# Second-kind layers: who scales the wide part of the fourth batch's probabilities

## The reference, cut to what matters

```python
def hybrid_layer(x, ...):
    z = rms_norm_2(x, norm_g) @ w_in
    o_a = fox_attention(...)    * silu(f_gate)     # 4 heads, causal, with decay
    o_b = conformer_conv(...)   * silu(c_gate)     # 31 taps, layer norm, silu, product
    o_c = nsa_attention(...)    * silu(n_gate)     # 8 heads in 2 groups of 4
    return x + concatenate([o_a, o_b, o_c]) @ w_out

# inside the attentions, for every head and every query token q:
p = softmax(scores[q, keys <= q])                  # masked
o = p @ v
# nsa: o = gate0 * o_compressed + gate1 * o_selected + gate2 * o_window
```

## Time and profile before

| what | value |
|---|---|
| median of three executions | 1596.06 us |
| the profiled execution | 1593.2 us |
| its span, first to last instruction | 1591.4 us |
| TensorE busy | 1577.7 us, 99% |
| VectorE busy | 1058.8 us, 67% |
| ScalarE busy | 832.8 us, 52% |
| GpSimd busy | 259.6 us, 16% |

### The profile page before, as it was taken

One profiled execution on the slowest core, in us unless ns is written; L12 is line 12 of the kernel. 1 busy time (PEld: TensorE's weight loads), 2 busy tenths in 40 slices (PEclk: granted clock), 3 DMA queues, 4 the chain that ended last, 5 costly groups with the idle time before them and its releaser, 6 DMA issues.

```text
span 1591.4 us, 27283 instructions
## 1 busy us (share of the span) xinstructions
PE 1577.7 (99%) x11244; PEld 1434.2 (90%) x11244; DVE 1058.8 (67%) x1263; ACT 832.8 (52%) x1143; POOL 259.6 (16%) x207
## 2 busy tenths in 40 slices
PE   9999999999999999999999999999999999999998
PEld 9999888898989999999988889899999998879886
DVE  5555557865865555655565777576555589978996
ACT  5443456753454444544455665345444475757584
POOL 0000061010000000000015001000000039804960
PEclk9999999999999999999999999999999999999999
DMA  7657565442555655556746543355665557146712
GB/s 255 215 186 226 185 194 160 129 155 83 183 185 186 209 185 185 178 196 204 236 159 195 159 152 107 119 176 166 207 201 187 169 164 237 58 140 192 232 34 93
DMA packets 207813, 273.99 MB, mean 172 GB/s; under 512 B 18822, under 2 KB 168168, under 8 KB 207208
## 3 DMA queue, kind: packets, MB, share of 16 engines
q1 hardware_dynamic: 207576, 272.67, 53.7%
q10 hardware_dynamic: 144, 0.00, 0.0%
HBM read 271.61 MB, written 1.08 MB: 171 GB/s over the span
## 4 chain that ended last, share of the span: by engine, by line
PE 96%; DVE 2%; ACT 1%; issue 0%; POOL 0%; POOLq 0%; ACTq 0%; DVEq 0%
PE bank L571 30%; PE bank L620 15%; PE bank L1063 9%; PE bank L1052 7%; PE bank L2128 6%; PE bank L1256 4%; PE bank L1338 3%; PE bank L2106 3%; PE bank L2381 3%; PE bank L2281 1%; PE bank L1198 1%; PE bank L1034 1%; PE bank L1171 1%; PE bank L2213 1%; PE bank L2240 1%; PE bank L1138 1%
## 5 line engine op out<-in xcount | busy, mean ns | idle before, releaser
L483 DVE TENSOR_TENSOR wlo<-raw,whi 128x2048 fp32r<-128x2048 f32 (+1 forms) x255 | 576.5, 2264 | 307.1 <-ACT whi L472 306.6
L472 ACT ACTIVATE whi<-raw 128x2048 fp32r<-128x2048 f32 (+2 forms) x257 | 482.8, 1881 | 277.1 <-PE bank L620 102.1
L571 PE MATMUL bank<-hT_hi,whi 128*128 128x256 f32 x1408 | 390.7, 277 | 0.0
L571 PE MATMUL bank<-hT_lo,whi 128*128 128x256 f32 x1408 | 389.6, 277 | 0.0
L571 PE MATMUL bank<-hT_hi,wlo 128*128 128x256 f32 x1408 | 389.5, 277 | 0.0
L571 PEld LDWEIGHTS bank<-hT_lo,whi 128*128 128x128 f32 x1408 | 265.0, 188 | 0.0
L571 PEld LDWEIGHTS bank<-hT_hi,whi 128*128 128x128 f32 x1408 | 264.3, 188 | 0.3 <-DVE wlo L446 0.2
L571 PEld LDWEIGHTS bank<-hT_hi,wlo 128*128 128x128 f32 x1408 | 264.3, 188 | 0.0
L620 PE MATMUL bank<-whi,Y 128*128 128x512 f32 (+1 forms) x748 | 224.5, 377 | 0.0
L620 PEld LDWEIGHTS bank<-whi,Y 128*128 128x128 f32 x748 | 140.1, 188 | 27.9
L326 POOL TENSOR_TENSOR st<-st 128x1 f32<-128x1 f32 x17 | 14.0, 833 | 914.4 <-ACT X L319 914.4
(11 more groups left out here) (411 smaller groups left out, 2837.9 us busy)
## 6 DMA issues: line engine op xcount, KB each, us to landing
raw<-in_ffn_w SPq DMA_DIRECT2D x131, 1024.0 KB, 5.3
raw<-in_w_in SPq DMA_DIRECT2D x80, 1024.0 KB, 5.3
raw<-in_w_out SPq DMA_DIRECT2D x16, 1024.0 KB, 4.9
raw<-in_w_br_na SPq DMA_DIRECT2D x4, 1024.0 KB, 5.0
raw<-in_w_br_mla SPq DMA_DIRECT2D x4, 1024.0 KB, 5.0
raw<-in_w_br_gla SPq DMA_DIRECT2D x4, 1024.0 KB, 5.0
raw<-in_cmp_k_w SPq DMA_DIRECT2D x4, 1024.0 KB, 5.4
raw<-in_cmp_v_w SPq DMA_DIRECT2D x4, 1024.0 KB, 6.1
```

The lines of the kernel that those rows point to most:

```text
L472: act.activation(m["whi"][:, slot, 0:w], m["raw"][:, slot, 0:w], ACT.Copy).then_inc(s.hi_ready, 1)
L483: dve.tensor_tensor(m["wlo"][:, slot, 0:w], m["raw"][:, slot, 0:w], m["whi"][:, slot, 0:w].bitcast(F32), ALU.subtract).then_inc(s.lo_ready, 1)
L571: mm = pe.matmul(B[bank][:, mt * T:(mt + 1) * T], a, b, start=(n == 0 and k == 0), stop=(n == KK - 1 and k == 2))
```

## The change

Batch 3 joins the batches whose wide part ScalarE scales. VectorE's `prob.3` no longer issues line 2734, and ScalarE gets a step `prob.3` between `turn.7` and `exp.12`. It holds for both second-kind layers.

```diff
@@ -1945,7 +1945,7 @@ ACT2
-    ln_square tall.8 turn.7 exp.12 turn.8 exp.13 turn.9 exp.14 ln_tanh turn.10-11 out.1 ln_high hi.22 turn.12-14 hi.23
+    ln_square tall.8 turn.7 prob.3 exp.12 turn.8 exp.13 turn.9 exp.14 ln_tanh turn.10-11 out.1 ln_high hi.22 turn.12-14 hi.23
@@ -1963,7 +1963,7 @@
-WIDE_ON_SCALAR = (1, 2)
+WIDE_ON_SCALAR = (1, 2, 3)
```

## The result

The changed kernel takes 1599.02 us at the median (1595.22 to 1600.02, nine executions), against 1594.58 us for the kernel before in the same series (1593.49 to 1596.32, nine). The ratio is 1.0023, 95% interval [1.0015, 1.0032]: 3.7 us slower, 2.4 to 5.1 us by the interval (the two medians alone differ by 4.4). The forecast was 3.20 us more, or 1599.3 us in all, counted from a base of 1596.06 us. With nine executions that base stands at 1594.58, 1.5 us lower.

What follows compares the result with a forecast made beforehand. The prediction took TensorE as the bound (busy 99% of the span), with no slack against ScalarE's queue at `value.2`. Removed 0, added 1.60 us per layer over two layers: 1596.06 + 3.20 = 1599.3 us, range 1595.9 to 1600.9.

Steps and rivals of the forecast that it cites:

- The removal is worth 0: VectorE's `prob.3`: dropping line 2734, 1.22 us per layer, saves nothing because `ln.0` behind it waits for TensorE.
- 1.60 us added per layer: ScalarE's queue between `turn.7` and `exp.12`: four added activations delay `turn.8`, and so `value.2`, by 1.60 us.
- The wait at `turn.9` lies inside the one at `value.2`: TensorE: `turn.9` starts 0.44 us late for batch 3's wide part, which adds nothing to the delay of `value.2`.
- rival 3: TensorE: the new wait at `turn.9` adds to the one at `value.2`; 4.1 us slower, 1600.1 us; chance 8 in 100.
- So nothing behind `value.2` adds to the delay: TensorE after `value.2`: blocks run with inputs ready, other engines move along, so 1.60 us per layer neither grows nor shrinks.
- the cover at `turn.12`: Slack between the end of VectorE's `prob.4` and TensorE's loads of `turn.12`: claimed to grow from 0.81 to 1.04 us.
- The time in all, 1599.3 us: Whole kernel: median of three timed executions, 1596.06 us, plus 3.20 us.
- The sign for the first output product: Second layer, line 2381 on TensorE: start moves from 1556.31 by 3.20 us to 1559.51.
- Rival 1: TensorE's hidden waits further on take the delay back; between nothing and about 2.5 us left, 1596.1 to 1598.6; chance 17 in 100.
- Rival 2: VectorE's queue decides at `turn.12`, so its saving counts: up to 2.44 us faster, 1593.6 us; chance 5 in 100.
- The difference of the two engines' times alone: Scaling batch 3's wide part, priced by rule only: 2 x (1.60 - 1.22) = 0.8 us slower; the prediction rejected it.

Runs made afterwards that it cites:

- ScalarE's part alone: Kernel before plus ScalarE's four activations per layer, written to spare columns, while VectorE keeps scaling batch 3's wide part: 1.0029, 4.6 us over before.
- the gap filled: Changed kernel plus four extra TensorE products of 128 columns, which nobody reads, between `turn.9` and `value.2` in both layers: 1.0020 and 1.0018 against before.
- the earlier place: Changed kernel with ScalarE's `prob.3` behind `turn.6`, where `hi.21` stood, and `hi.21` moved behind `exp.14`: 1.0003 against before.
- the doubled part: Changed kernel plus four more ScalarE activations of the same size, to spare columns, ahead of its `prob.3`: 1.0060, 9.6 us over before.

## Why the prediction was right, and what it lacked

- **The removal is worth 0**: right. VectorE idles that much longer before `ln.0`, and taking line 2734 away alone gives 0.9999. With ScalarE's part alone, which keeps line 2734, `value.2` starts as late as in the changed kernel.
- **1.60 us added per layer**: right. It measured 1.59, and 1.58 with the gap filled. Half the work gives 0.79, twice the work 3.16 (8.65 - 5.49): the wait follows ScalarE's queue one to one.
- **The wait at `turn.9` lies inside the one at `value.2`** (rival 3): right, it did not add. `turn.9` starts 5.20 us behind `ln.0` where it was 4.75, so it is 0.45 us late as forecast (0.44). The idle time shown before it is shorter, since its loads overlapped the ones ahead of them before.
- **"So nothing behind `value.2` adds to the delay"**: this step failed, though what was listed there held: no load behind `value.2` waits for another engine, and the cover at `turn.12` is 1.05 us (forecast 1.04). I looked there only for instructions that would be late and not at how fast TensorE would run after a pause. The clock fell behind `value.2` in four of the six layers seen, at 1.42 or 1.64 us each. As a mean over the layers that is about 2 x 4/6 x 1.6 = 2.1 us, which with the 3.2 makes 5.3; the two series of timed executions gave 3.7 (2.4 to 5.1) and 5.4 (3.3 to 7.3). By the mean clocks it falls less often, about once per execution, which makes some 3.2 + 1.6 = 4.8. So the number came out near, but the forecast's sum of 3.20 was only the part that is paid always.
- **The time in all, 1599.3 us**: it came within 0.3 us of the median by luck. The base was 1.5 us too high and the term for the clock was missing, and the two errors nearly cancel. The sign for the first output product (1559.51) had no such help: it starts at 1562.26.
- **Rival 1, the delay is taken back later**: it did not happen. With the clock held, the times were 3.2 and 2.9 us over before.
- **Rival 2, faster**: excluded by the removal alone.
- **The difference of the two engines' times alone** would have given 0.8 us. The place in the queue decided, as forecast: in the earlier place ScalarE's 1.60 us cost nothing at all, and here they cost all of themselves and more. The place is what counts and not the engine's rate.

The Trainium skill, TensorE: Matmul & The Clock Gate, section Why this matters for your kernels, advises against idle gaps of TensorE between bursts of products, since its clock then falls back. The traces agree, with 0.50 granted after a gap of 1.46 us. The row of the Trainium skill is written for longer gaps than that one, and here the measurement decides. The filled gap shows what the advice is worth here: some 1.5 us for each fall avoided.

What stays open is when exactly a gap makes the clock fall. After 0.28 and 1.46 us it fell four times in six, after 1.82 us two times in two, after 1.87 and 1.15 or 1.45 us (the doubled part) two in two, after 1.03 us not in four, and after 0.76 us not in two. The two outcomes of the same gap were not told apart by anything that I looked at in the trace. How often it falls in executions that were not profiled is an estimate from their rounded mean clocks and their times.

## What to carry to other kernels

Price work that you move onto an engine by the place in its queue: the same four activations cost 0 in front of a wait and 1.6 us per layer behind it. When a change makes TensorE stand still for longer than it did (here 1.46 us; 1.03 us did no harm in four layers), put a second term in the sum for its clock, and expect a spread from one execution to the next, since the same gap can cost it or not. Where such a gap can't be avoided, halving it or filling it with products that nobody reads kept the clock here.

## What the runs showed of the hardware

- A pause of TensorE of 1.46 us halved its granted clock for more than three microseconds in some layers and not in others, with all waits equal to 0.01 us. The fall began anywhere from 0.4 us before TensorE's next loads to 0.7 us behind them, and cost 1.42 to 1.64 us.
- Four useless products of 128 columns in the pause made the layer shorter than one whose clock fell by 1.43 to 1.64 us (9.83 against 11.26 and 11.47).
- An idle time shown before a weight load is not all to be gained: removing a wait of 0.24 us shortened the stretch by 0.06.
